# A decoder trunk on one core: an early load of the router's bias, a later wait for half of the tokens, and eight identity products between the router's products

## The reference

```python
logits = (tok @ router_w) + router_b
probs = jax.nn.softmax(logits, axis=-1)
top_p, top_i = lax.top_k(probs, TOP_K)          # TOP_K = 2
top_p = top_p / jnp.sum(top_p, axis=-1, keepdims=True)
gate = jnp.sum(jax.nn.one_hot(top_i, N_EXPERTS) * top_p[..., None], axis=1)
for ex in range(N_EXPERTS):                      # 8 experts, each 1024 -> 2 x 3584 -> 1024
    y = y + gate[:, ex:ex + 1] * swiglu(tok, w_gate_up[ex], w_down[ex])
h = h + rms_norm(y, m_post_norm)
```

## Time and profile before

| | |
|---|---|
| median of 3 runs | 1352.91 us (1350.77 to 1357.46) |
| the profiled execution | 1353.34 us, span 1351.4 us |
| busy: PE, PEld, DVE, ACT, POOL | 95%, 55%, 31%, 26%, 4% of the span |
| mean granted clock of TensorE | 0.99 of full |
| moved from and to memory | 424.34 MB, mean 314 GB/s |
| first expert product (L934) | at 507.72 us |

### The profile page before, as it was taken

The page is one execution under the profiler, slowest core; times in us unless marked ns, Lnnn a source line. Parts: engine busy times, 40 slices in busy tenths (PEclk is TensorE's granted clock), DMA queues, the critical chain, the costliest instruction groups (busy, mean ns, idle before and its releaser), DMA issues.

```text
span 1351.4 us, 26213 instructions
## 1 busy us (share of the span) xinstructions
PE 1290.0 (95%) x11388; PEld 744.0 (55%) x11388; DVE 422.1 (31%) x807; ACT 347.6 (26%) x660; POOL 50.6 (4%) x77
## 2 busy tenths in 40 slices
PE   8989999999889989999999999999999989999986
PEld 7988999999788873443343443333443332343331
DVE  7785866653697731001010001000001000000102
ACT  7886544443567630000000000000000000000001
POOL 3001100001120010000000000000000000000000
PEclk9999999999999979999999999999999999999999
DMA  9538455555223398999999999999999999999994
GB/s 288 166 97 265 127 186 183 162 185 161 69 96 110 116 376 320 356 366 397 417 418 418 416 417 419 416 418 419 415 417 419 416 418 419 416 418 418 417 418 186
DMA packets 128133, 424.34 MB, mean 314 GB/s; under 512 B 8321, under 2 KB 77185, under 8 KB 99345
## 3 DMA queue, kind: packets, MB, share of 16 engines
q1 hardware_dynamic: 127664, 421.58, 80.4%
q0 software_dynamic: 352, 1.06, 0.2%
HBM read 421.56 MB, written 1.05 MB: 313 GB/s over the span
## 4 chain that ended last, share of the span: by engine, by line
PE 70%; SPq 13%; DMA 7%; DVE 5%; ACT 3%; issue 2%; DVEq 0%; POOL 0%; ACTq 0%
PE bank L934 29%; SPq L1058 12%; PE bank L911 10%; PE bank L530 9%; PE bank L532 8%; PE bank L531 8%; DMA ring_low<-in_m_w_gate_up 4%; DMA ring_low<-in_m_w_down 2%; PE bank L889 1%; PE bank L870 1%; PE bank L901 1%; PE bank L903 1%; DMA rbias<-in_gain_rows 1%; DVE w_lo L1579 1%; ACT w_hi L1181 1%
## 5 line engine op out<-in xcount | busy, mean ns | idle before, releaser
L934 PE MATMUL bank<-ring_low,x_T 128*32 128x512 f32 (+1 forms) x3552 | 344.1, 541 | 9.4 <-DMA ring_low<-in_m_w_gate_up 8.1
L934 PEld LDWEIGHTS bank<-ring_low,x_T 128*32 128x32 f32 x3552 | 113.3, 110 | 234.3 <-issue 210.5
L911 PE MATMUL bank<-ring_low,eT 128*32 128x512 f32 x1632 | 182.4, 594 | 11.9 <-DMA ring_low<-in_m_w_down 11.9
L530 PE MATMUL bank<-u_hi,w_hi 128*128 128x272 f32 (+1 forms) x568 | 166.4, 293 | 7.0 <-DVE u_lo L1634 5.1
L1579 DVE TENSOR_TENSOR w_lo<-raw,w_hi 128x2048 fp32r<-128x2048 f32 (+7 forms) x89 | 143.9, 1638 | 93.6 <-ACT w_hi L1181 93.4
L532 PE MATMUL bank<-u_hi,w_lo 128*128 128x272 f32 (+1 forms) x568 | 164.2, 289 | 0.0
L531 PE MATMUL bank<-u_lo,w_hi 128*128 128x272 f32 (+1 forms) x568 | 163.5, 288 | 0.0
L2072 DVE TENSOR_TENSOR e_h<-bank,e_h 128x512 f32<-128x512 f32 (+1 forms) x40 | 22.7, 618 | 416.9 <-PE bank L934 416.9
L934 PE MATMUL bank<-ring_high,x_T 128*32 128x384 f32 (+1 forms) x1568 | 149.8, 536 | 0.0
L1181 ACT CAST w_hi<-raw 128x2048 fp32r<-128x2048 f32 (+7 forms) x89 | 117.9, 1352 | 52.9 <-PE bank L532 52.9
L911 PEld LDWEIGHTS bank<-ring_low,eT 128*32 128x32 f32 x1632 | 50.1, 110 | 135.1 <-issue 111.9
(11 more groups left out here) (321 smaller groups left out, 1353.0 us busy)
## 6 DMA issues: line engine op xcount, KB each, us to landing
ring_low<-in_m_w_gate_up SPq DMA_DIRECT2D x92, 1024.0 KB, 23.1
ring_low<-in_m_w_down SPq DMA_DIRECT2D x80, 1024.0 KB, 23.8
ring_low<-in_m_w_gate_up SPq DMA_DIRECT2D x88, 768.0 KB, 22.0
ring_high<-in_m_w_gate_up SPq DMA_DIRECT2D x36, 1024.0 KB, 24.5
ring_high<-in_m_w_down SPq DMA_DIRECT2D x32, 1024.0 KB, 24.7
ring_high<-in_m_w_gate_up SPq DMA_DIRECT2D x40, 768.0 KB, 21.8
raw<-in_f_w_gate_up SPq DMA_DIRECT2D x24, 1024.0 KB, 5.3
raw<-in_f_w_down SPq DMA_DIRECT2D x12, 1024.0 KB, 5.2
```

The lines of the kernel that those rows point to most:

```text
L530: nc.tensor.matmul(o, a[0], b[0], start=start, stop=False)
L911: return nc.tensor.matmul(strip(q, t, NT), eT[u][:, bank, P * i + GROUP * at:P * i + GROUP * at + GROUP], w[:, n, :], start=start, stop=stop)
L934: last = nc.tensor.matmul(strip(q + 3 * (kind_of == "up"), t, width), x_T[:, part, group(g)], w[:, width * n:width * n + width], start=(pa ...
```

## The change

It does four things.

1. `rbias` is loaded by the first instruction of POOL's list, with a semaphore of its own (`in_bias`), and VectorE waits for that one before L1945. The buffer is taken ahead of the stage buffers, so that nothing shares its place.
2. `grow` is loaded where it was, with the semaphore `in_grow`; VectorE waits for it only after the last expert, before it applies the gain.
3. Between the router's products, behind every second slice k, TensorE issues a product of the identity with 256 columns of the constants into bank 7 (four for each block of tokens, eight in all). Nobody reads them.
4. In each expert TensorE waits for VectorE's half of x at weight piece 4 instead of piece 0.

```diff
@@ -276,6 +276,7 @@
         gw = sb("gw", [P, KD, NE])
         weight = sb("weight", [P, NB * NE])[:, :]
         first = sb("first", [P, NB * NE])[:, :]
+        rbias = sb("rbias", [P, NE])
         banks = [ctx.enter_context(nc.psum_tensor(f"bank{i}", [P, 512], F32)) for i in range(8)]
 
         def pr(name, c=None):
@@ -368,7 +369,6 @@
         u_tok = sb("u_tok", [P, NB, D])
         queue = sb("queue", [P, 3, NB, NE])
         queue_next = sb("queue_next", [P, 3, NB, NE])
-        rbias = sb("rbias", [P, NE])
         rt = sb("rt", [P, 10, 3 * NE])[:, :, 0:NB * NE]
         rounds_i = sb("rounds_i", [1, 1], I32)
         order_i = sb("order_i", [1, NE], I32)
@@ -395,7 +395,8 @@
         landed = [sem(f"landed{i}") for i in range(RAW)]
         ring_landed = [sem(f"ring_landed{i}") for i in range(LANDINGS)]
         hi_done, lo_done = sem("hi_done"), sem("lo_done")
-        in_const, in_par, in_rows, in_ident = sem("in_const"), sem("in_par"), sem("in_rows"), sem("in_ident")
+        in_const, in_par, in_bias, in_grow, in_ident = (
+            sem("in_const"), sem("in_par"), sem("in_bias"), sem("in_grow"), sem("in_ident"))
         in_x = [sem(f"in_x{b}") for b in range(3)]
         x_sum, x_root, x_scaled = sem("x_sum"), sem("x_root"), [sem(f"x_scaled{b}") for b in range(3)]
         pe_done = sem("pe_done")
@@ -814,6 +815,8 @@
                     pe.wait_ge(*((hT_by_dve if k >= 4 else hT_by_act), b + 1))
                     nc.tensor.matmul(banks[6][:, NE * b:NE * b + NE], hT[:, k, t0:t0 + n], gw[:, k, :],
                                      start=False, stop=False)
+                    if k % 2:
+                        nc.tensor.matmul(banks[7][:, 0:256], ident, con[:, 0:256], start=True, stop=True)
             last = nc.tensor.matmul(banks[6][:, 0:NB * NE], ones, zeros, start=False, stop=True)
             mark(last, "logits")
             keep_busy(2, 4)
@@ -916,9 +919,10 @@
                     if kind_of != "down":
                         if c == 0:
                             pe.wait_ge(x_by_act, ex * 4 + 4)
-                            pe.wait_ge(x_by_dve, ex * 4 + 4)
                             if kind == BIG:
                                 pe.wait_ge(scatter_added, it * 4 + 4)
+                        if c == 4:
+                            pe.wait_ge(x_by_dve, ex * 4 + 4)
                         if c == GATE_END[1] - 7:
                             pe.wait_ge(silu_done, it * EH_PAIR + EH_BEFORE[kind] + ng)
                         if c == UP_END[0] - 7 and kind == BIG:
@@ -1090,6 +1094,7 @@
                 steps[0] += 1
                 pool.wait_ge(pool_link, steps[0])
 
+            pool.dma_start(rbias[:], gain_rows[0:1, D:D + NE].to_broadcast([P, NE])).then_inc(in_bias, 16)
             pool.wait_ge(in_par, 16)
             pool.wait_ge(dve_step, 2)
             link(nc.gpsimd.tensor_scalar(lt[0], pr("lam"), -1.0, 0.0, ALU.mult, ALU.max))
@@ -1151,8 +1156,7 @@
             at(pool, "weighed", HEADS - 1)
             pool.dma_start(post_gain, gain_row[0:1, :].to_broadcast([P, D])).then_inc(in_gain, 16)
             at(pool, "chunk", CH[("b_out", 3)])
-            pool.dma_start(grow[:], gain_rows[0:1, 0:D].to_broadcast([P, D])).then_inc(in_rows, 16)
-            pool.dma_start(rbias[:], gain_rows[0:1, D:D + NE].to_broadcast([P, NE])).then_inc(in_rows, 16)
+            pool.dma_start(grow[:], gain_rows[0:1, 0:D].to_broadcast([P, D])).then_inc(in_grow, 16)
 
             at(pool, "logits")
             for part in range(2):
@@ -1940,7 +1944,7 @@
             def wide(x):
                 return x[:, :, None].to_broadcast([P, NB, NE])
 
-            dve.wait_ge(in_rows, 32)
+            dve.wait_ge(in_bias, 16)
             dve.wait_ge(h_summed, 2 * NB)
             nc.vector.tensor_reduce(mss, halves.rearrange("p (b h) -> p b h", h=2), AX_X, ALU.add).then_inc(h_sum, 1)
             dve.wait_ge(rstd_t, 1)
@@ -2100,6 +2104,8 @@
                 y = acc[:, b, NT * n:NT * n + NT]
                 nc.vector.tensor_tensor(y, banks[i][:, :], y, ALU.add).then_inc(added, 1)
 
+            dve.wait_ge(in_grow, 16)
+
             def with_gain(i):
                 n, b = i // NB, i % NB
                 c = slice(NT * n, NT * n + NT)
```

## The result

| | before | after |
|---|---|---|
| median | 1351.84 us (1349.32 to 1357.46, 4 runs) | **1339.33 us** (1336.93 to 1340.61, 4 runs) |
| ratio | | 0.990 (95%: 0.9865 to 0.9934) |
| span of the profiled execution | 1351.4 us | 1337.2 us (the execution 1339.2 us) |
| first expert product | 507.72 us | 504.85 us by the chain, 504.78 in the timeline |

The kernel became 12.5 us faster; 2.7 were forecast, and the range ended at 1346.5. Of the 14.2 us between the two spans, 2.9 lie ahead of the first expert, the amount that was forecast. The other 11.3 are gained behind it, where the forecast saw no change.

The account below looks back on a forecast made before the run. The weight stream, hanging on the first expert's start at 507.72 us, was taken to set the end. Terms: -0.9 (router) -1.0 (gather) -1.05 (copies) +0.2 (early load) = -2.75 us, giving 1350.2 us beside the median; range 1346.5 to 1355.5.

Parts of the forecast that it names:

- The frame: Whole kernel: the weight stream sets the end and hangs on the first expert's start, whose shift passes on whole.
- part 1: Bias load moved to POOL's queue head: VectorE's wait at L1945 vanishes, 2.8 us gained if left alone; buffer shift priced nothing.
- The early load: Kernel start: the moved bias load competes with the first weight chunk; 0.2 us lost.
- Part 2: Router: eight identity products at full clock lengthen it from 4.8 to 6.96 us; L1951 still 0.9 us earlier than before.
- Part 3: Gather before the first expert: the clock falls while it runs, so 6.0 us instead of 6.97; 1.0 us gained.
- a fall at 390.1 us: Evidence for the gather's clock: it fell 1.5 us after TensorE resumed from a 3.27 us wait, not after 1.60 us.
- Part 4: First expert: waiting for VectorE's half of x at weight piece 4 hides its copies; 1.05 us gained.
- The clock held through the gather: Rival: the clock stays up, the gather takes 3.55 us, the expert starts at 502.35; 1347.7 us, chance 0.22.
- The products at half clock: Rival: the eight products don't hold the router's clock and run at half; 1354.7 us, slower than before, chance 0.20.
- The end that does not move with the start: Rival: the late stream has a fixed beginning, or the start moves under 1 us; 1352.9 us, chance 0.11.

Follow-up runs that it names:

- e1_place_only: Kernel before with only the rbias buffer taken ahead of the stage buffers, putting ring_low at byte 24832; 1342.1 us beside 1355.16, ratio 0.991.
- e15_identity_16: Changed kernel with the eight identity products cut from 256 to 16 columns; 1342.62 us beside 1356.22, ratio 0.9893.
- e4_before_64: Kernel before with the buffer small 32 bytes shorter, ring_low at byte 24768 (multiple of 64), ring_high kept; 1352.55 us beside 1355.16, ratio 0.9993.
- e7_no_identity: Changed kernel without the eight identity products; 1339.76 us beside 1354.39, ratio 0.9892.
- e8_wait_at_0: Changed kernel with the wait for VectorE's half of x back at weight piece 0; 1340.15 us beside 1354.39, ratio 0.9891.
- e13_low_256: Changed kernel with gw written over router_w and a pad, ring_low at byte 24576 (multiple of 256), ring_high kept; 1339.15 us, ratio 0.9896.
- e12_low_128: Changed kernel with gw written over router_w and pads, ring_low at byte 24704 (multiple of 128), ring_high kept; 1350.3 us, ratio 0.9973.
- e6_after_high_256: Changed kernel with 192 unused bytes ahead of ring_high, which lies at byte 187904 (multiple of 256); 1339.8 us, ratio 0.9893.

## Why the prediction was wrong, and where it was right

**The frame** was right: the end hangs on the stream, and the stream on the first expert's start. At one rate a start moves the span about one to one: 506.29 and 1338.2 us in e1_place_only, 504.78 and 1337.2 in the changed kernel, 508.09 and 1340.3 in e15_identity_16. The DMA engines still wait for TensorE behind the start (65 and 300 GB/s in 505 to 515 us, where the earlier trace rows has 2 and 185).

**The step that failed** stands in part 1: "The rbias buffer also moves 32 bytes down and shifts what lies behind it; no row prices that. ... so I take nothing." The row used for it, 421 GB/s for both rings together in the earlier trace rows, was read at one place of the buffers only and can't say what another place gives. (It is also a stretch of 5 us; over 700 to 1100 us the rate is 417.) The cost was unknown and should have been bounded like the others: the settled stream lasts 686 us, so each percent of its rate is 7 us, more than twice the whole sum. It measured 11.3 us by the rate; e1_place_only, with the moved buffer alone, is 13 us faster in the medians.

**Part 1, the bias wait**: gone, as forecast. The early load was put at 0.2 us; the token block came 0.9 later, and the router's first product 0.65 later (487.49 for 486.84 in the earlier trace rows), whatever the cause of that. The 2.8 us of gain rest on a bias load of 10.1 us; with the 8.7 and 8.8 us that it took in e1_place_only and e4_before_64 the wait ends 1.3 to 1.4 us sooner after the first product. Against those two builds the bias sum of the changed kernel, 7.51 us after the first product, comes 0.6 to 0.7 later, not earlier.

**Part 2, the eight products**: the clock stayed full from 487 to 495, as forecast. The bias sum was due 7.31 us after the first product and came after 7.51. Forecast at 494.15, it starts at 495.00: 0.65 from the late start and 0.20 from the products. From there to the gather it took 4.44 us, the forecast's figure to the hundredth. What was mis-sized is the kernel without them: it was put at 5.46 us from first product to bias sum, and e7_no_identity took 6.35, with the keep-busy products at half clock in the way of the positions. The clock fell about 1.3 us after the first product there and about 2.2 in the kernel before. So beside e7_no_identity the products cost 1.2, not 1.9.

**Part 3, the clock in the gather**: it fell inside the gather (0.78, then 0.65), as forecast; 5.41 us instead of 6.0, so 1.56 gained instead of 1.0. The argument was weaker than its outcome. It rested on a fall at 390.1 us behind a wait of 3.27 us; the changed kernel has a wait of 3.24 us at the same place, and its clock stayed at 1.00 to 393 us. The length of a wait doesn't decide it alone.

**Part 4, the moved wait**: 1.05 forecast, 1.26 in the chain (the earlier trace rows against 504.85 us), 1.35 in e8_wait_at_0.

The start therefore moved by 0.05 + 1.56 + 1.26 = 2.87 us, where 2.9 was forecast: a router 0.85 later than expected, made up by the gather (0.6) and the copies (0.2). That the start came out so close is partly luck: it lies at 507.72, 506.29 and 504.74 us in the three builds with the schedule of before, and between 504.27 (e13_low_256) and 507.88 us (e12_low_128) in those with all four edits. What the edits are worth in the whole time is not told from zero by these runs.

**The rivals.** The clock held through the gather: no. The products at half clock: no, but e15_identity_16 shows that mechanism, with a fall near 490.5 and a first expert 3.3 us later. The end that does not move with the start: no. The case that happened, a stream with another rate, was not among them; all three took the stream as fixed.

**The new idle of TensorE** was not foreseen. It is in every build with eight more products (8.0 to 9.3 us with `ring_low` well placed, 11.2 to 11.5 with it ill placed) and in none without them (before, e1, e4, e7). It costs nothing so far: without it TensorE waits 11.6 us for weights (8.8 + 2.8 in e7_no_identity) instead of 0.8, and the ends differ only by their starts. What makes it is not shown; that the turn of the loop waits for instructions is an argument. For it speaks the queue in the page that carries instructions. It moves 92 transfers in each of the four builds without the idle, and 95 in 13 of the 15 with it (94 in the other two), about as many more as there are turns. First the kernel before, then the changed one:

```profile
q8 instruction: 92, 1.51, 0.5%
q8 instruction: 95, 1.56, 0.4%
```

e7_no_identity and e15_identity_16 show that the idle goes with the eight instructions and not with their work; no run adds others in their stead, and none moves the loop.

## What to carry to other kernels

An edit that adds or moves a buffer moves every buffer behind it: look up where the destinations of the long stream land before and after, and keep them at multiples of 256 bytes. Where a stream sets the end, give its rate a term of its own in the sum and a rival of its own; 1.7 percent of it outweighed all that the moved waits won. To test an edit's schedule, hold the buffers' places fixed with pads.

A step that one trace shows may be a step of that trace alone. Here the stage that the forecast was built on took 20.88, 19.81 and 18.11 us in three builds with the same waits and products. Before a gain of 1 to 3 us is read from such a stage, look at it in a second build.

## What the runs showed of the hardware

- A stream of 768 to 1024 KB transfers runs at 424 GB/s with 71% of its bytes going to a buffer at a multiple of 256 bytes, and at 417 to 418 at the other places tried; 420 with only the other 29% so placed.
- Eight products of 256 columns between products of 8 held the granted clock at full for 8 us; of 16 columns they did not (0.54 in 490 to 496 us).
- A 4 KB load issued by GpSimd at the head of the kernel held up a token block by 0.9 us.
- Eight more products ahead of a loop brought TensorE an idle of 2 to 5 us at each of three turns, with 256 or 16 columns alike.
- A gather of 32 records took 5.41 us or 6.9 to 7.0 in builds with the same work ahead of it, as the granted clock fell within it or just before it (1.3 us into it in the changed kernel, 0.1 us before it in e6_after_high_256).
- A 4 KB load behind the full stream took 10.1, 8.7, 8.8 and 9.4 us from issue to landing in four builds.
